# Output gate of a hybrid encoder layer: projection by rounded high and low parts in 512-column products

## The reference

```python
h = layer_norm(x, emb_ln_g, emb_ln_b)
proj = h @ w_in[l]                      # 256 x 1024 @ 1024 x 3328
q_a, k_a, v_a, q_h, i_h, zf_fwd, zf_bwd, z_g = jnp.split(proj, IN_SPLITS, axis=-1)
attn = windowed_gqa(q_a, k_a, v_a, sink)
o = (forward + backward gated linear recurrence of q_h, i_h, zf_fwd, zf_bwd)
o = o * lax.rsqrt(jnp.mean(jnp.square(o), axis=-1, keepdims=True) + RMS_EPS)
rec = o.reshape(b, s, HGRN_WIDTH) * norm_g * jax.nn.silu(z_g)
mix = jnp.concatenate([attn, rec], axis=-1) @ w_out[l]
h = layer_norm(DEEPNORM_ALPHA * h + mix, ln1_g[l], ln1_b[l])
ffn = top-4-of-32 mixture of experts: for each expert (h @ w_up[e]), clamped SwiGLU, @ w_down[e]
h = layer_norm(DEEPNORM_ALPHA * h + ffn, ln2_g[l], ln2_b[l])
```

## Time and profile before

| | us |
|---|---|
| median of 3 runs | 1087.07 (1087.04 to 1087.44) |
| the profiled execution, its own time | 1087.5 |
| its span, first to last instruction | 1085.8 |
| TensorE busy | 1037.2 (96%) |
| VectorE busy | 256.9 (24%) |
| ScalarE busy | 194.5 (18%) |
| moved by DMA | 428.34 MB, mean 395 GB/s |

### The profile page before, as it was taken

The page is one execution under the profiler, slowest core; times in us unless marked ns, Lnnn a source line. Parts: engine busy times, 40 slices in busy tenths (PEclk is TensorE's granted clock), DMA queues, the critical chain, the costliest instruction groups (busy, mean ns, idle before and its releaser), DMA issues.

```text
span 1085.8 us, 12732 instructions
## 1 busy us (share of the span) xinstructions
PE 1037.2 (96%) x5174; PEld 454.8 (42%) x5174; DVE 256.9 (24%) x670; ACT 194.5 (18%) x366; POOL 8.0 (1%) x25
## 2 busy tenths in 40 slices
PE   8999999999999999999999999999999998899995
PEld 8988664333333333333333333333333333333331
DVE  6886463111111111111111111101111111111113
ACT  5674221111111111111110111101111111011110
POOL 2000000000000000000000000000000000000000
PEclk9999999999999999999999999999999999999999
DMA  9826897999999999999999999999999999999993
GB/s 326 233 68 181 350 409 311 411 426 428 430 433 432 427 435 430 430 432 429 429 435 428 429 434 431 432 432 428 434 433 427 432 432 428 434 430 425 427 422 158
DMA packets 36464, 428.34 MB, mean 395 GB/s; under 512 B 3952, under 2 KB 17312, under 8 KB 20320
## 3 DMA queue, kind: packets, MB, share of 16 engines
q1 hardware_dynamic: 34848, 427.17, 94.1%
q10 hardware_dynamic: 1568, 0.44, 0.2%
HBM read 426.03 MB, written 1.05 MB: 393 GB/s over the span
## 4 chain that ended last, share of the span: by engine, by line
PE 64%; DMA 34%; DVE 1%; ACT 0%; issue 0%; DVEq 0%; SPq 0%; ACTq 0%
DMA ring<-in_w_down_dram 23%; PE bank L1606 23%; PE bank L1672 15%; DMA wbuf<-in_w_down_dram 7%; PE bank L1556 4%; PE bank L1288 4%; DMA tail_mem<-in_w_down_dram 4%; PE bank L1541 3%; PE bank L1305 3%; PE bank L1351 3%; PE bank L1549 1%; PE bank L1650 1%; PE bank L1617 1%; PE bank L1636 1%; PE bank L1333 1%; PE bank L1269 0%
## 5 line engine op out<-in xcount | busy, mean ns | idle before, releaser
L1606 PE MATMUL bank<-ring,wbuf 128*64 128x512 f32 x1248 | 278.1, 595 | 1.3 <-DMA ring<-in_w_up_dram 1.3
L1672 PE MATMUL bank<-ring,wbuf 128*64 128x512 f32 x640 | 151.9, 628 | 19.8 <-DMA ring<-in_w_down_dram 19.0
L1606 PEld LDWEIGHTS bank<-ring,wbuf 128*64 128x64 f32 x1248 | 87.5, 137 | 162.9 <-issue 151.9
L715 ACT ACTIVATE wbuf<-wbuf 128x256 f32<-128x256 f32 x64 | 26.7, 416 | 450.8 <-DVE wbuf L1213 450.8
L1672 PEld LDWEIGHTS bank<-ring,wbuf 128*64 128x64 f32 x640 | 51.7, 144 | 117.0 <-issue 113.2
L1197 DVE TENSOR_SCALAR hT<-iota_s,hT 128x128 f32<-128x128 f32 x64 | 19.3, 343 | 340.1 <-PE bank L1636 339.8
L1213 DVE TENSOR_SCALAR wbuf<-bank 128x256 f32<-128x256 f32 x64 | 26.9, 420 | 304.9 <-PE bank L1606 304.9
L1606 PE MATMUL bank<-tail_mem,wbuf 128*64 128x512 f32 x416 | 93.0, 594 | 0.0
L1606 PE MATMUL bank<-wbuf 128*64 128x512 f32 x384 | 85.8, 594 | 0.0
L1556 PE MATMUL bank<-wbuf,putT 64*128 64x512 f32 x264 | 65.6, 616 | 0.7 <-ACT wbuf L720 0.7
L1541 PE MATMUL bank<-X,hT 128*64 128x512 f32 x256 | 60.9, 593 | 0.0
(11 more groups left out here) (264 smaller groups left out, 811.4 us busy)
## 6 DMA issues: line engine op xcount, KB each, us to landing
ring<-in_w_up_dram SPq DMA_DIRECT2D x29, 4096.0 KB, 40.0
ring<-in_w_down_dram SPq DMA_DIRECT2D x14, 4096.0 KB, 37.6
ring<-in_w_up_dram SPq DMA_DIRECT2D x20, 2048.0 KB, 14.6
wbuf<-in_w_up_dram SPq DMA_DIRECT2D x10, 4096.0 KB, 40.0
tail_mem<-in_w_up_dram SPq DMA_DIRECT2D x9, 4096.0 KB, 40.5
wbuf<-in_w_down_dram SPq DMA_DIRECT2D x5, 4096.0 KB, 36.4
ring<-in_w_down_dram SPq DMA_DIRECT2D x8, 2048.0 KB, 14.0
tail_mem<-in_w_up_dram SPq DMA_DIRECT2D x8, 2048.0 KB, 19.0
```

The lines of the kernel that those rows point to most:

```text
L715: a.activation(sig[:, w], glu[:, w], ACT.Sigmoid, scale=SIG_ALPHA).then_inc(s["sig_ready"], 1)
L1606: ins = mm(bank[n][c * SLOTS:(c + 1) * SLOTS, :], xT[:, k, :], units(row, n, c), start=(k == 0), stop=(k == KT - 1))
L1672: ins = mm(bank[1 if last else 2][c * SLOTS:(c + 1) * SLOTS, :], actT[:, at:at + SLOTS], wk[:, a * D + c * 512:a * D + (c + 1) * 512], sta ...
```

## The change

The zg projection is computed by rounded parts too, for both units together. A new step ("zg", i, 0) does product i of three (high x high, weights high x hidden low, weights low x hidden high), each 16 matmuls with a moving operand of 512 columns (two blocks of 256). Product 0 stands where unit 0 was, product 1 after kpT(1), ahead of aT, product 2 where unit 1 was. The high parts of the weights go into places 1 and 4 of `wbuf` (those of qh's first and ih's second unit), the low parts over the raw weights, the high part of `hT` into the two recurrence arrays `k` and `C` of direction 1, the low part over `hT`. ACT gets two casts of 128x2048 and two of 128x1024, DVE two subtractions of 128x1024 and two of 128x2048. `w_out` for the recurrence now has its place only when all of zg is done.

```diff
-    UNITS = [(n, h) for n, _, w in GROUPS for h in range(w // 256)]
+    UNITS = [(n, h) for n, _, w in GROUPS for h in (range(w // 256) if n != "zg" else (1, 0))]
...
+        slots_r = wbuf_r[:, :, :].rearrange("p c (a k n) -> p (c a) k n", a=2, k=KT)
+        zg_high, zg_low = slots_r[:, 1:5:3], slots_r[:, 0:6:5]
+        z_high = halves_r[:, 6, :].rearrange("p (k n) -> p k n", k=KT)
...
-        STEPS += [("proj", "zg", 0)] + two("kpT", 1) + two("aT", 0) + two("aT", 1) + [("lnT", 0, 0)] + two("pT", 3)
-        STEPS += [("proj", "zg", 1), ("pv", 1, 0), ("kv", 0, 0), ("kv", 1, 0)]
+        STEPS += [("zg", 0, 0)] + two("kpT", 1) + [("zg", 1, 0)] + two("aT", 0) + two("aT", 1) + [("lnT", 0, 0)] + two("pT", 3)
+        STEPS += [("zg", 2, 0), ("pv", 1, 0), ("kv", 0, 0), ("kv", 1, 0)]
...
-            sp.wait_ge(s["proj_done"], len(UNITS) - 1)
-            sp.dma_start(wbuf[:, 2, :].rearrange("p (k n) -> p k n", k=4), w_out_v[:, 4:8, :]).then_inc(s["wout_in"], 16)
             job_is_done(sp, ("aT", 1, TT - 1))
             load_chunk(sp, 2)
+            sp.wait_ge(s["proj_done"], len(UNITS))
+            sp.dma_start(wbuf[:, 2, :].rearrange("p (k n) -> p k n", k=4), w_out_v[:, 4:8, :]).then_inc(s["wrec_in"], 16)
+            load_chunk(sp, 3)
             sp.wait_ge(s["bup_split"], 4)
             sp.wait_ge(s["zeroed"], 1)
             sp.dma_start(bup, bsplit).then_inc(s["bup_in"], 16)
-            load_chunk(sp, 3)
-            sp.wait_ge(s["proj_done"], len(UNITS))
...
             def sig_out(t):
-                unit_is_done(act, "zg")
+                act.wait_ge(s["proj_done"], len(UNITS) - 1 + t)
...
             exps(1)
+
+            def zg_rounded(h, u, freed):
+
+                act.wait_ge(win_in[u % WBUF], 16 * (u // WBUF + 1))
+                act.wait_ge(s["proj_done"], freed + 1)
+                a.copy(zg_high[:, h], w_raw(u).rearrange("p (k n) -> p k n", k=KT)).then_inc(s["zg_high_ready"], 1)
+
+            zg_rounded(0, UI["zg", 0], UI["qh", 0])
             attended(0)
             probs(3)
+            act.wait_ge(s["aT_ready"], 4)
+            for i in range(2):
+                a.copy(z_high[:, 4 * i:4 * i + 4, :], hT[:, 4 * i:4 * i + 4, :]).then_inc(s["z_high_ready"], 1)
+            zg_rounded(1, UI["zg", 1], UI["ih", 1])
             probs_turned(2)
...
             v.tensor_copy(ih[:, 1, :], proj_bank("ih", 1)[:, :]).then_inc(proj_read[GI["ih"]], 1)
+            for i in range(2):
+                dve.wait_ge(s["z_high_ready"], i + 1)
+                k4 = slice(4 * i, 4 * i + 4)
+                v.tensor_tensor(hT_r[:, k4, :], hT[:, k4, :], z_high[:, k4, :].bitcast(F32),
+                                ALU.subtract).then_inc(s["z_low_ready"], 1)
+            for h in range(2):
+                dve.wait_ge(s["zg_high_ready"], h + 1)
+                v.tensor_tensor(zg_low[:, h], w_raw(UI["zg", h]).rearrange("p (k n) -> p k n", k=KT),
+                                zg_high[:, h].bitcast(F32), ALU.subtract).then_inc(s["zg_low_ready"], 1)
             shared(3)
...
+            def zg_products(i):
+
+                wp, hp = ((zg_high, z_high), (zg_high, hT_r), (zg_low, z_high))[i]
+                if i == 0:
+                    pe.wait_ge(proj_read[GI["zg"] - 2], 1)
+                    pe.wait_ge(s["zg_high_ready"], 2)
+                    pe.wait_ge(s["z_high_ready"], 2)
+                elif i == 1:
+                    pe.wait_ge(s["z_low_ready"], 2)
+                else:
+                    pe.wait_ge(s["zg_low_ready"], 2)
+                for t in range(TT):
+                    for k in range(KT):
+                        ins = mm(proj_bank("zg", t)[:, :].rearrange("p (h n) -> p h n", h=2), hp[:, k, t * P:(t + 1) * P],
+                                 wp[:, :, k, :], start=(i == 0 and k == 0), stop=(i == 2 and k == KT - 1))
+                    if i == 2:
+                        ins.then_inc(s["proj_done"], 1)
...
-                    pe.wait_ge(s["wout_in"], 48)
+                    pe.wait_ge(s["wout_in"], 32)
...
                     else:
+                        pe.wait_ge(s["wrec_in"], 16)
                         job_is_read(pe, ("catT", 2 + t, 0))
```

More of the change, by code:

```diff
@@ L88, in encoder_layer @@
                 nc.sbuf_tensor("wbuf_r", [P, WBUF // 2, 4096], F32R) as wbuf_r, \
-                nc.sbuf_tensor("hT_r", [P, KT, TOK], F32R), \
+                nc.sbuf_tensor("hT_r", [P, KT, TOK], F32R) as hT_r, \
                 nc.sbuf_tensor("X_r", [P, TT, D], F32R), \
@@ L232, in encoder_layer @@
         names = ("x_in0 x_in1 emb_in rows_in ln1_in ln2_in par_in "
-                 "wout_in bias_in braw_in bias_left bup_split bup_in zeroed consts h_ready lb_ps proj_done job_done logf_ready logf_in exps_in "
+                 "wout_in wrec_in bias_in braw_in bias_left bup_split bup_in zeroed consts h_ready lb_ps proj_done job_done logf_ready logf_in exps_in "
                  "k_ready var_ready std_ready zg_sig mx_ready prob_ready prob_shared rec_cat rms_std mix_half "
-                 "mix_done hT_params h_high_ready h_low_ready w_high_ready w_low_ready ln1rows_in gsum_in router_in pre_ready x1_ready logit_done top_ready g4_ready mask_ready gate_ready "
+                 "mix_done hT_params h_high_ready h_low_ready w_high_ready w_low_ready zg_high_ready zg_low_ready z_high_ready z_low_ready ln1rows_in gsum_in router_in pre_ready x1_ready logit_done top_ready g4_ready mask_ready gate_ready "
                  "rank_done ex_ready route_done key_ready sel_ready plan_ps plan_ready lbm_ready lb_exp "
@@ L276, in encoder_layer @@
         STEPS += two("x1T", 0) + two("x1T", 1) + two("logit", 0) + two("logit", 1)
-        jobs = [x for x in STEPS if x[0] not in ("first", "proj", "mix", "logit")]
+        jobs = [x for x in STEPS if x[0] not in ("first", "proj", "zg", "mix", "logit")]
         J = {j: n for n, j in enumerate(jobs)}
@@ L1413, in _ @@
                     project(d, i)
+                    continue
+                if kind == "zg":
+                    zg_products(d)
                     continue
```

## The result

The changed kernel takes 1104.48 us (median of 4, 1103.56 to 1106.78), the kernel before 1087.26 in the same comparison: slower by 1.55%, ratio 1.0155, 95% interval 1.0142 to 1.0168. The forecast was 1100.3 with a range of 1094.5 to 1105. The profiled execution of the changed kernel took 1105.35 us with a span of 1103.5, 17.7 us more than the span before.

What follows compares the result with a forecast made beforehand. The expert stage is a full-rate DMA stream started by TensorE at pass 0; the bias copy also sets that. Copy landing at 128.8, states, and 1.8 us clock loss put o 13.2 us later: 1100.3 us, range 1094.5 to 1105.

Steps and rivals of the forecast that it cites:

- The chain of the argument: TensorE's arrival at pass 0 moves the expert stream and the end equally; the bias copy's landing also sets that arrival.
- First wait: Before aT(1,0), TensorE stands still 5.4 us until 108.0, for the bank that k_turned(1) frees behind ScalarE's late bias casts.
- The products: In zg, 48 matmuls of 512 columns at 0.22 us replace 14.0 us: 3.4 us less (2.3 to 8.1).
- The queue: In SP's list, the bias copy behind chunk 2, `w_out` and chunk 3 lands 19.4 us after 109.4, at 128.8.
- the clock loss after the first wait: TensorE's lower clock after the wait before aT(1), said to be hidden behind the bias copy's landing.
- The clock after the second wait: From kv(·,2) to o's second half, after TensorE stands still 7.3 us, the lower clock costs 1.8 us (0 to 1.9).
- My row: Profile row behind the clock term: after a 2.58 us wait, 32 matmuls took 8.57 us against 6.87, 1.7 us lost.
- The sum: o's second half starts at 138.7 instead of 125.53, 13.2 us later, and the end moves with it: 1100.3 us.
- A: Rival at SP's queue: the bias copy does not queue and lands 8.9 us after its issue; 1096.6 us, chance 0.08.
- B: Rival at aT(1): no first wait, the copy lands at 123.1; +7.5 us, 1094.6, chance 0.06.
- C: Rival: product 2 ends 3.4 us earlier and nothing else is late; faster, 1083.7 us, chance 0.04.

Runs made afterwards that it cites:

- e8: The kernel before with half of the last zg unit left out (4 of 8 blocks of the width): 1089.88 us against 1089.06, ratio 1.0009.
- e1: The kernel before with only the change's order of SP's queue, products in f32 and no casts: 1099.87 us against 1088.04, ratio 1.0111.
- e2: The changed kernel with the bias copy issued ahead of `w_out` and chunk 3: 1092.5 us against 1088.04 for the kernel before, ratio 1.0039.
- e3: The changed kernel with VectorE's first `bias_rest` moved ahead of the copy of ih: 1098.18 us against 1088.04 for the kernel before, ratio 1.0093.
- e4: The changed kernel with both the bias copy and the first `bias_rest` moved early: 1086.04 us against 1088.04 for the kernel before, ratio 0.9982.
- e6: The changed kernel with the bias copy between `w_out` and chunk 3: 1101.04 us against 1089.06 for the kernel before, ratio 1.0114.
- e5: The changed kernel with 38 products of the identity ahead of kv(·,2): 1104.71 us against 1089.06 for the kernel before, ratio 1.0149.

## Why the prediction was right

*The chain of the argument.* That the end follows TensorE's arrival at pass 0, and that this follows the second half of o, held to 0.1 us: both came 16.8 us later. That a gain of TensorE alone would be lost was shown by e8, and that the copy's landing decides, by e1 and e2.

*First wait.* Forecast 5.4 us until 108.0; measured 4.6 until 107.91, product 1 and aT(0) having ended later. The cause was as told: e3 takes away only VectorE's lateness, and the wait is gone. chunk 2's issue: forecast 109.4, measured 109.93.

*The products.* Forecast 0.22 us each, measured 0.235 for the first 16 (3.76 us from start to start), 0.239 for those of product 1 and 0.240 for those of product 2 at full clock (e3): 11.3 to 11.5 us for 48 instead of 10.6. At 512 columns in fp32r a product costs nearly twice one of 256 (0.122), close to the upper bound. So the whole gain to be had was 2.1 us (e4), not 3.4.

*The queue, the term that was mis-sized most.* Forecast 19.4 us from chunk 2's issue to the copy's landing, measured 131.71 - 109.93 = 21.8, inside its bounds of 18.4 and 23.1. With chunk 2's issue 0.5 us late, the landing came 2.9 us after the forecast 128.8. Half of this, 1.45 us, is that zg ended at 116.75 and not at 115.3, and `w_out` and chunk 3 wait for that. The forecast had left 1.3 us for the lower clock in zg's end; it took 2.1 (lnT and pT 1.83 us instead of 1.01, product 2 5.10 instead of 3.84, both against e3). The rest is aT(1)'s end, 0.4, and the products, 0.3. The other half is mainly the step that `w_out` and chunk 3 are issued "while chunk 2 still flows", each costing only its bytes. Chunk 2 did land after their issue (119.0), but it was nearly out of bytes: DMA moved 197 GB/s from 116 to 117 and 49 from 117 to 118. `w_out` then took 7.9 us to land, as long as a load out of an idle DMA was forecast to take (8.0), chunk 3 landed 5.6 us behind it and the copy 1.3 us behind that. That is 14.9 us from `w_out`'s issue, where the forecast had 128.8 - 115.4 = 13.4. I had called the clock loss after the first wait hidden; it isn't, as these loads wait for zg's end.

*The clock after the second wait.* Forecast 1.8 us with an upper bound of 1.9; measured 9.25 - 6.78 = 2.5 in the changed kernel, and by the same subtraction 2.3 in e1, 2.4 in e6 and 1.9 in e3. My row (8.57 against 6.87) came after a wait of 2.58 us and was no upper bound. e5 shows that 2.0 of the 2.5 us are the clock's; at full clock the other 0.5 would be spent waiting for VectorE's states (7.27 against 6.78). The worked example of the Trainium skill ("TensorE: Matmul & The Clock Gate", "HAM oscillation"), about 0.8 us for a gap by the prediction's estimate from it, was further off than the row.

*The sum.* 14.8 us for the copy's landing (forecast 11.9) and 2.5 for the clock (1.8), less 0.5 that TensorE's own way had as slack before, are the 16.8 us of the second half of o (13.2). The forecast was 4.2 us short of the measured median, and 3.6 of it are these two terms. The mechanism was right, but the size was near its limit: the measured median lies 0.5 us under the upper end of the range, and the clock's term lies above its own bound.

*The rivals.* A (the copy passes the queue) falls: it landed 13.8 us after its issue, 9.6 with one chunk less ahead (e6) and 4.1 with neither load ahead (e2). B is what e3 makes (10.1 us where 7.5 were forecast for it), and C is what both moves make: with neither wait the products do gain, though 2 us and not 3.4. The parts nearly add up. Counted from e4, which has neither, the first wait costs 6.5 us (e2, 4.5 above the kernel before), the order of SP's list 12.1 (e3, 10.1 above it), and both together 19.2 (the changed kernel, 17.2 above it). The difference of 0.6 us is inside the runs' intervals.

## What to carry to other kernels

Where a transfer releases an engine, ask what is ahead of it in its queue and what the issuing list waits for, not how long it takes itself: 0.5 MB behind 4 MB cost 12 us (e3 against e4, the clock's part included), and the same copy issued first held nothing up. When work is added to an engine with idle time, follow who waits for the instruction behind it: 6.9 us on VectorE cost VectorE nothing, and stopped TensorE through two casts of ScalarE. And before a busy engine is relieved, look for a second chain that arrives at the same moment; here a removal of 3.5 us gained nothing by itself (e8), and the products' 2 us were gained only when neither chain was late (e4).

## What the runs showed of the hardware that was not expected

What a wait of TensorE cost at the lower clock did not follow from its length. Ahead of kv(·,2) it was 2.5 us after 8.75 us of standing still, 1.9 after 9.47 (e3) and 2.4 after 4.0 (e6); in the row of before it was 1.7 after 2.58; and after the 3.18 us of e8 it was nothing, with a granted clock of 1.00. The same first wait of 4.6 to 4.7 us was followed by 8.84 us from aT(1) to pv(1) in the changed kernel, 8.23 in e2 and 7.40 in e6, where the same work takes 5.9 at full clock (estimated from e3: half of aT's 2.02, 1.01 and 3.84). So one row gives neither a lower nor an upper bound. The loss was avoided by products of the identity during the wait (granted clock 1.00 in e5).

An fp32r product of 128x128 weights and 512 columns takes 0.235 to 0.240 us from start to start, one of 256 columns 0.122, and for product 2 it makes no difference whether the 512 columns are one block or two.
